# Squares summed over partitions in three bf16 parts instead of one f32 product, in a hybrid decoder block

## The reference

```python
h = rmsnorm(x, norm_g)
q_g, k_g, v_g, gk_lr, gate_g, u_p, gate_p, q_m, gate_m = split(h @ w_in)
gk = log_sigmoid(gk_lr @ w_gk_up + b_gk) / 16
o_gla = rmsnorm(gla_chunked(q_g, k_g, v_g, gk), gla_norm_g) * silu(gate_g)   # 4 heads of 128, chunks of 64
o_pool = (multiscale_pool(u_p) @ pool_w) * pool_scale * silu(gate_p)         # windows 2, 4, 8, 16
o_mem = memory_attention(q_m, rmsnorm(mem), w_mem_kv) * silu(gate_m)         # 4 heads, 256 tokens
x = x + concat(o_gla, o_pool, o_mem) @ w_out
return rmsnorm(x, final_g)
```

## Time and profile before

| | |
|---|---|
| Median of 3 runs | 1385.68 us (1384.72 to 1386.30) |
| The profiled execution's own time | 1386.14 us |
| Its span, first to last instruction | 1384.3 us |
| Instructions | 35236 |
| Busy: PE, DVE, ACT, POOL | 98%, 58%, 54%, 27% |
| Mean granted TensorE clock | 0.998 |

### The profile page before, as it was taken

The page is one execution under the profiler, slowest core; times in us unless marked ns, Lnnn a source line. Parts: engine busy times, 40 slices in busy tenths (PEclk is TensorE's granted clock), DMA queues, the critical chain, the costliest instruction groups (busy, mean ns, idle before and its releaser), DMA issues.

```text
span 1384.3 us, 35236 instructions
## 1 busy us (share of the span) xinstructions
PE 1357.1 (98%) x14716; PEld 1015.7 (73%) x14716; DVE 796.9 (58%) x1524; ACT 753.6 (54%) x1380; POOL 370.7 (27%) x313
## 2 busy tenths in 40 slices
PE   6999999999999999999999999999999999999997
PEld 5788668576695968769586785958768596876953
DVE  5876567575554654554555555565555455555454
ACT  7886545655545464454646545464554556455352
POOL 2120164135323142332223223222332313233100
PEclk9999999999999999999999999999999999999999
DMA  9476556663673737456383654638366373745731
GB/s 387 174 209 214 213 183 215 199 242 137 203 255 94 275 107 260 183 180 240 95 294 123 242 201 147 251 97 290 132 209 249 116 265 97 262 177 183 254 83 46
DMA packets 143623, 269.31 MB, mean 195 GB/s; under 512 B 75137, under 2 KB 88705, under 8 KB 140417
## 3 DMA queue, kind: packets, MB, share of 16 engines
q1 hardware_dynamic: 142768, 266.20, 56.3%
q10 hardware_dynamic: 720, 1.06, 0.2%
HBM read 220.03 MB, written 30.41 MB: 181 GB/s over the span
## 4 chain that ended last, share of the span: by engine, by line
PE 94%; DVE 3%; ACT 2%; DMA 1%; issue 0%; SPq 0%; DVEq 0%; ACTq 0%
PE bank L665 34%; PE bank L704 33%; PE bank L683 10%; PE bank L892 2%; PE bank L918 2%; PE bank L912 2%; PE bank L926 2%; PE bank L971 2%; PE bank L994 2%; PE bank L903 1%; PE bank L780 1%; PE bank L876 1%; DMA out_parts<-fg 1%; PE bank L607 1%; DVE arena L1578 1%; PE bank L764 1%
## 5 line engine op out<-in xcount | busy, mean ns | idle before, releaser
L665 PE MATMUL bank<-ring,arena 128*128 128x512 f16 x1440 | 318.4, 379 | 0.0
L665 PEld LDWEIGHTS bank<-ring,arena 128*128 128x128 f16 x1440 | 138.5, 98 | 165.6 <-issue 5.9
L704 PE MATMUL bank<-arena,ring 128*128 128x128 f16 x4032 | 237.1, 219 | 0.0
L704 PE MATMUL bank<-arena,wres 128*128 128x128 f16 x4032 | 237.0, 219 | 0.0
L704 PEld LDWEIGHTS bank<-arena,ring 128*128 128x128 f16 x4032 | 228.4, 98 | 5.2 <-DVE arena L1556 1.9
L704 PEld LDWEIGHTS bank<-arena,wres 128*128 128x128 f16 x4032 | 227.7, 98 | 2.5 <-issue 2.5
L665 PE MATMUL bank<-wv,arena 128*128 128x512 f16 x768 | 170.2, 382 | 1.1 <-DVE wv L1542 1.1
L2029 POOL TENSOR_TENSOR arena<-arena 128x1024 f32<-128x1024 f32 (+2 forms) x42 | 64.8, 1543 | 355.1 <-ACT arena L1042 352.9
L665 PEld LDWEIGHTS bank<-wv,arena 128*128 128x128 f16 x768 | 75.5, 98 | 91.3 <-issue 2.3
L2037 POOL TENSOR_TENSOR arena<-arena 128x1024 f16<-128x1024 f32 x32 | 67.5, 2131 | 200.1 <-ACT arena L1060 200.1
L1637 DVE SCALAR_TENSOR_TENSOR arena<-bank,sca,arena 128x512 f32<-128x512 f32 x60 | 45.0, 749 | 111.1 <-DMA arena<-in_x 92.2
(11 more groups left out here) (247 smaller groups left out, 2004.6 us busy)
## 6 DMA issues: line engine op xcount, KB each, us to landing
ring<-out_parts SPq DMA_DIRECT2D x120, 512.0 KB, 5.5
ring<-gate_parts SPq DMA_DIRECT2D x92, 512.0 KB, 5.8
ring<-side_parts SPq DMA_DIRECT2D x92, 512.0 KB, 6.5
arena<-in_xt SPq DMA_DIRECT2D x16, 1024.0 KB, 6.8
arena<-in_x SPq DMA_DIRECT2D x32, 512.0 KB, 4.4
out<-arena SPq DMA_DIRECT2D x31, 512.0 KB, 2.9
arena<-in_w_out SPq DMA_DIRECT2D x16, 512.0 KB, 5.4
out_parts<-arena SPq DMA_DIRECT2D x6, 512.0 KB, 6.7
```

What stands on the lines that cost most here:

```text
L665: mm = nc.tensor.matmul(ap, lhs, rhs, start=k == 0 and n == 0, stop=(k, n) == last)
L704: mm = nc.tensor.matmul(ap, w[:, p, k, j * P:(j + 1) * P], x_part(r, b)[:, k, :], start=fresh and j == 0 and k == 0 and n == 0, stop=k == ...
```

## The change

For the heads in blocks 1 to 14 and for the next x in blocks 4 to 14 the f32 squares are split into three bf16 numbers each (high part, middle part, rest), and three bf16 products with a bf16 matrix of ones are summed in PSUM in place of the one f32 product. For the heads ACT squares PSUM a second time with a bf16 output (`o_part[p][0]`, after waiting for the block's transposes, whose source lies in the same memory), DVE subtracts it from `osq`, ACT copies the difference to bf16 (`o_part[p][1]`), DVE subtracts again into `o_part[p][2]`. The order is: on ACT square and high part of each head in turn, then both middle parts, ahead of the copies SG3 and SG1; on DVE both first subtractions and both second ones, ahead of the third row add. For the next x the same four steps work on 256 columns: on ACT the high part stands before PM's second copy and the middle part behind it; on DVE the subtractions stand before and behind PM's `add_12`. The matrix `ident16`, which nothing read, gives way to `ones16`.

```diff
--- before.py
+++ after.py
@@ -123,7 +123,7 @@
         wlr = sb("wlr", [P, KT, 2 * RANK], F16)
         arena = sb("arena", [P, O_END // 4], F32)
         ident = sb("ident", [P, P], F32)
-        ident16 = sb("ident16", [P, P], F16)
+        ones16 = sb("ones16", [P, P], BF16)
         ones = sb("ones", [P, P], F32)
         causal = sb("causal", [P, P], F32)
         keep = sb("keep", [P, TB], BF16)
@@ -188,6 +188,7 @@
         kd = view(O_KD, [NPAIR, TB], F32)
         ke = view(O_KE, [NPAIR, TB], F32)
         osq = [view(o, [2, TB], F32) for o in (O_KD, O_KE)]
+        o_part = [[view(O_T + 3072 * p + 1024 * n, [2, TB], BF16) for n in range(3)] for p in range(2)]
         v = view(O_V, [NT, 512], F32)
         gate = view(O_GATE, [KT, TB], F32)
         mhl = view(O_MHL, [2, KT, TB], F16)
@@ -218,6 +219,7 @@
         pwb = view(O_QM, [2, P], F32)
         rmem = view(O_QM + 1024, [NMEM], F32)
         msq = sq
+        x_sum = [sq[:, 4 + n, :].bitcast(BF16)[:, 0:TB] for n in range(3)]
         sums = xs[:, 1, :, :, :].rearrange("p r b c -> p (r b c)")
         shade = {QK: wres[:, 0:2, :].rearrange("p s c -> p (s c)")[:, 0:4 * (512 + RANK)].rearrange(
                      "p (k c) -> p k c", k=4),
@@ -351,8 +353,10 @@
             sem(n) for n in ("sT_ok", "max_ok", "nmax_ok", "rs_ok", "s_ok", "xn_ok", "og_ok",
                              "mix_g", "mix_m", "mix_p", "mmax_ok", "m_lo"))
 
+        xsq_hi, xsq_rest, xsq_mid, xsq_lo = (sem(n) for n in ("xsq_hi", "xsq_rest", "xsq_mid", "xsq_lo"))
         w_sum, halo_ok, sq_add, p_lo, x_lo, m_all, s_carry, sg_ok = (
             sem(n) for n in ("w_sum", "halo_ok", "sq_add", "p_lo", "x_lo", "m_all", "s_carry", "sg_ok"))
+        osq_hi, osq_rest, osq_mid, osq_lo = (sem(n) for n in ("osq_hi", "osq_rest", "osq_mid", "osq_lo"))
         m_st, sc_ok, cut_ok = (sem(n) for n in ("m_st", "sc_ok", "cut_ok"))
         d_tail = [sem(f"d_tail{t}") for t in range(NT)]
         half_max, y_gain, y_end = (sem(n) for n in ("half_max", "y_gain", "y_end"))
@@ -606,6 +610,14 @@
                 pe.wait_ge(sq_add, 3 * (n + 1))
                 nc.tensor.matmul(bank[3][:, 0:TB], ones[:, :], sq[:, 0, :], start=True, stop=True).then_inc(pe_rb, 1)
 
+            def rms_parts(n):
+
+                pe.wait_ge(xsq_mid, n - WHOLE)
+                pe.wait_ge(xsq_lo, n - WHOLE)
+                for k in range(3):
+                    mm = nc.tensor.matmul(bank[3][:, 0:TB], ones16[:, :], x_sum[k], start=k == 0, stop=k == 2)
+                mm.then_inc(pe_rb, 1)
+
             def total(g):
 
                 pe.wait_ge(w_sq, 2 * (g + 1))
@@ -848,7 +860,7 @@
                     phase(i, PM, 2)
                     pe.wait_ge(ad[GG], 4 * (i + 1))
                     if not last:
-                        rms_sum(i + 1)
+                        rms_parts(i + 1)
                     pe.wait_ge(ad[QK], 4 * (i + 1))
                     values(0).then_inc(pe_v, 1)
                     values(1).then_inc(pe_v, 1)
@@ -922,9 +934,16 @@
 
                 def head_ms(p):
 
-                    pe.wait_ge(o_sq, 2 * i + p + 1)
-                    nc.tensor.matmul(bank[6 + p][:, :], ones[:, :], osq[p], start=True,
-                                     stop=True).then_inc(pe_msq, 1)
+                    if first or last:
+                        pe.wait_ge(o_sq, 2 * i + p + 1)
+                        nc.tensor.matmul(bank[6 + p][:, :], ones[:, :], osq[p], start=True,
+                                         stop=True).then_inc(pe_msq, 1)
+                        return
+                    pe.wait_ge(osq_mid, 2 * i + p - 1)
+                    pe.wait_ge(osq_lo, 2 * i + p - 1)
+                    for n in range(3):
+                        mm = nc.tensor.matmul(bank[6 + p][:, :], ones16[:, :], o_part[p][n], start=n == 0, stop=n == 2)
+                    mm.then_inc(pe_msq, 1)
 
                 def quarter(n):
                     if not first:
@@ -1332,7 +1351,13 @@
                     act.wait_ge(ad[GG], 4 * (i + 1))
                     early_copies(i, PM)
                     second_copy(i, UM)
+                    if not last:
+                        act.wait_ge(sq_add, 3 * (i + 2))
+                        nc.scalar.activation(x_sum[0], sq[:, 0, :], ACT.Copy).then_inc(xsq_hi, 1)
                     second_copy(i, PM)
+                    if not last:
+                        act.wait_ge(xsq_rest, i - WHOLE + 1)
+                        nc.scalar.activation(x_sum[1], sq[:, 0, :], ACT.Copy).then_inc(xsq_mid, 1)
                     third_copy(i, UM)
                     third_copy(i, PM)
                     qm_split()
@@ -1427,8 +1452,17 @@
                     if first:
                         act.wait_ge(cp[GG if p == 0 else PM], 4)
                         silu(p, GG if p == 0 else PM)
+                    elif not last:
+                        for turned in d_turn:
+                            act.wait_ge(turned, 32 * (i + 1))
+                        nc.scalar.activation(o_part[p][0], bank[b][:, :].rearrange("p (a t) -> p a t", a=2),
+                                             ACT.Square).then_inc(osq_hi, 1)
                 if first:
                     nc.scalar.preload_act_table_set(EXP_LN)
+                elif not last:
+                    for p in range(NPAIR):
+                        act.wait_ge(osq_rest, 2 * i + p - 1)
+                        nc.scalar.activation(o_part[p][1], osq[p], ACT.Copy).then_inc(osq_mid, 1)
                 if not last and not is_whole(i + 1):
                     x_mixed(i + 1, SG3)
                     x_mixed(i + 1, SG1)
@@ -1800,7 +1834,13 @@
                     mixed_lo(i - 1)
                     add_11(i, PM)
                     add_12(i, UM)
+                    if not last:
+                        dve.wait_ge(xsq_hi, i - WHOLE + 1)
+                        nc.vector.tensor_tensor(sq[:, 0, :], sq[:, 0, :], x_sum[0], ALU.subtract).then_inc(xsq_rest, 1)
                     add_12(i, PM)
+                    if not last:
+                        dve.wait_ge(xsq_mid, i - WHOLE + 1)
+                        nc.vector.tensor_tensor(x_sum[2], sq[:, 0, :], x_sum[1], ALU.subtract).then_inc(xsq_lo, 1)
                     add_2(i, UM)
                     add_2(i, PM)
 
@@ -1936,6 +1976,20 @@
                     norm_rows(i - 1, 0)
                 if not last:
                     dve.wait_ge(xn_ok, 2 * (i + 2))
+                def osq_rest_of(p):
+                    dve.wait_ge(o_sq, 2 * i + p + 1)
+                    dve.wait_ge(osq_hi, 2 * i + p - 1)
+                    nc.vector.tensor_tensor(osq[p], osq[p], o_part[p][0], ALU.subtract).then_inc(osq_rest, 1)
+
+                def osq_lo_of(p):
+                    dve.wait_ge(osq_mid, 2 * i + p - 1)
+                    nc.vector.tensor_tensor(o_part[p][2], osq[p], o_part[p][1], ALU.subtract).then_inc(osq_lo, 1)
+
+                if not first and not last:
+                    osq_rest_of(0)
+                    osq_rest_of(1)
+                    osq_lo_of(0)
+                    osq_lo_of(1)
                 if not last:
                     rows(2)
                 if first:
@@ -2019,7 +2073,7 @@
                                     pattern=[[1, P]], channel_multiplier=-1).then_inc(ident_ok, 1)
             pool.wait_ge(ident_ok, 4)
             nc.gpsimd.memset(causal[0:64, 64:128], 0.0).then_inc(built, 1)
-            nc.gpsimd.tensor_copy(ident16[:, :], ident[:, :]).then_inc(built, 1)
+            nc.gpsimd.memset(ones16[:, :], 1.0).then_inc(built, 1)
 
             def fold_rows(n0):
 
```

## The result

The changed kernel takes 1388.63 us (median of 13 runs, 1387.26 to 1390.73), the kernel before 1385.09 us (median of 13, 1384.19 to 1388.45) beside it. The ratio is 1.0022, with a 95% interval of 1.0015 to 1.0030: slower by 3.0 us by the ratio (2.1 to 4.2), by 3.5 us by the medians. 1388.4 us had been forecast.

What follows compares the result with a forecast made beforehand. TensorE, busy 98% of the span, was taken to bound the kernel. 10.6 us lost in blocks 1 and 2 less 7.9 gained elsewhere gave +2.7 on the median 1385.68, so 1388.4 us, range 1376.5 to 1393.0.

Steps and rivals of the forecast that it cites:

- TensorE's gain: Head sums in blocks 1 to 14 shorten by 0.51 us a block, next-x sums in blocks 4 to 14 by 0.16.
- Rival (d): On TensorE, three bf16 products cost what the f32 pass costs; the 7.9 us gain falls away, 1396 us; chance 0.05.
- The x chain: Blocks 4 to 14: ACT and DVE split x before TensorE's next-x sum, 0.3 us to spare, no cost.
- Rival (c): Low part of x late for TensorE's sum in blocks 4 to 14, 0.3 to 0.8 us a block; chance 0.12.
- The heads in blocks 3 to 14: Head subtractions end 3.3 us before TensorE asks; the spare before the logits shrinks to 0.39 us; no stall.
- The turns in blocks 1 and 2: New DVE subtractions alternate with GpSimd's weight combinations, 2.77 us a turn; TensorE stands 1.9 and 2.8 us.
- Rival (b): Blocks 1 and 2 don't stand, subtractions find gaps between GpSimd's operations; all is gained, 1376.8 us; chance 0.15.
- The clock: After the stands, one fall of TensorE's granted clock in each of blocks 1 and 2, 1.6 us on QK products.
- Rival (a): Turns in blocks 1 and 2 as said but the clock holds: 1385.3 us, no change; chance 0.16.
- the other bound: No fall of the clock in blocks 1 and 2, put at 3.1 us less.
- The sum: Blocks 1 and 2 lose 4.8 and 5.8 us, together 10.6; less 7.9 gained elsewhere, net +2.7 us.

Runs made afterwards that it cites:

- the run with late combinations: Changed kernel, but GpSimd's weight combinations wait for both head products of the block before, and plain copies replace DMA transposes: 1379.70 us, ratio 0.9965.

## Why the prediction was right, point by point

- **TensorE's gain.** x: 0.16 us a block forecast and measured. Heads: 0.51 forecast, 0.42 measured. This term was mis-sized: six products were put at 6 x 0.216 = 1.30 us, and the pair holds TensorE 1.39. The price of f16 held for bf16: the three of the first head take 0.65 in block 4 (the fourth product begins at 459.68). The last three hold TensorE 0.74 in blocks 1 and 2 (from 196.74 to 197.48), where they can be read apart, so 0.09 us lies between them and the low-rank product. What it is was not separated by a run. Over 12 blocks it made 7.9 us into 6.8. Rival (d), bf16 products as dear as f32, falls with these rows.
- **The x chain.** It passed with 0.5 us to spare, 0.3 forecast. In block 4 of the changed kernel the fold ends at 415.39; the high part, both subtractions and the window sum between them:

```profile
415.42 0.42 ACT L1356 ACTIVATE arena<-arena 128x256 bf16<-128x256 f32 x1 [3.16 <-POOL arena L2083]
...
415.87 0.84 DVE L1839 TENSOR_TENSOR arena<-arena 128x256 f32<-128x256 f32 x1 [3.09 <-ACT arena L1356]
...
417.20 0.74 DVE L1843 TENSOR_TENSOR arena<-arena 128x256 bf16<-128x256 f32 x1
...
415.35 1.09 POOL L2160 TENSOR_TENSOR arena<-arena 128x542 f32<-128x542 f32 x1
416.51 1.14 POOL L2162 TENSOR_TENSOR arena<-arena 128x538 f32<-128x538 f32 x1
```

  Both subtractions wait a turn, as forecast (0.84 and 0.74 us for 256 columns, where 0.4 was estimated without one), and the last is done at 417.94 for 418.46. Rival (c), slower by this chain, falls: no stand.
- **The heads in blocks 3 to 14.** No stand. In block 4 the last subtractions end at 455.78, 3.25 us before TensorE asks at 459.03; 3.3 were forecast. The copy that releases the logits ended at 464.59, the logits began at 465.00: 0.41 to spare, 0.39 forecast.

```profile
454.31 1.47 DVE L1986 TENSOR_TENSOR arena<-arena 128x512 bf16<-128x512 f32 x2
...
464.11 0.48 ACT L1204 ACTIVATE arena<-bank,sca 128x256 f32<-128x256 f32 x1 [0.60 <-DVE arena L1940]
465.00 1.08 PE L792 MATMUL bank<-arena,up 128*128 128x256 f32 x4
```

- **The turns in blocks 1 and 2.** Stands of 1.9 and 2.8 us were forecast; they were 1.77 and 2.73, 1.78 and 2.72. One turn was forecast at 2.77 us; two subtractions take 5.59, 2.8 each. The two blocks agree with each other within 0.01 us, so the mechanism was right here and not only the total. Rival (b), no turns, falls with the trace, and the run with late combinations shows that the turns are the cause, not only beside it.
- **The clock.** A fall in each, 1.6 us: 1.3 and 1.6 measured. That these falls come from the stands is read from the trace, and from the run with late combinations, where stands and falls are gone together; the falls were not tried apart from the stands. Rival (a), stands without falls, is out by the profiled execution; of the 13 runs none has a mean clock above its 0.997, and none is under 1387.26 us, where (a) gave 1385.3. That bound has a slip: the prediction's own logits times with and without a fall differ by 1.4 and 1.6 us, so the other bound was 3.0 us less and not 3.1; it moves no chance.
- **The sum.** +4.8 and +5.8 forecast for the two blocks, +4.5 and +5.9 measured. The net of +2.7 came out as +3.6 by the traces: 1.1 us less gain on the heads, 0.2 us less loss in the two blocks. By the medians it was +3.5, an error of 0.8 us. The median of before beside it was 0.6 us under the one that the forecast started from, which hid most of this. So it is luck that 1388.4 came within 0.2 us of 1388.63, where 0.8 us had been the honest miss; the mechanism and the sign are not luck.

## What to carry to other kernels

Before a DVE operation with two SBUF inputs is added, look in every stage for what GpSimd does at that time: where it has a row of long operations, each new one waited here for one of these whole (2.8 us for 0.7), and all that stands behind it in DVE's queue came later by as much. A change that is good in 12 of 14 blocks can lose in the other two more than it gains; left out there, the same change gives 0.995 (with copies for the transposes; with the transposes it was not run). A semaphore that holds GpSimd back moves the loss to whoever waits for GpSimd's results, so follow these to their last user first, DMA queue included.

## What the runs showed of the hardware

In the run with late combinations a scan takes turns too: two scans of 256 columns, 1.27 us together in the kernel before, take 5.41 us beside the combinations, and DVE's other operations with two SBUF inputs behind them 2.7 and 3.4 for 0.7 and 1.3.

```profile
208.37 5.41 DVE L1714 TENSOR_TENSOR_SCAN arena<-keep,arena 128x256 f32<-128x256 bf16 x2
213.82 2.66 DVE L1718 TENSOR_TENSOR arena<-arena 128x512 f32<-128x512 f32 x1
216.40 3.37 DVE L1561 SCALAR_TENSOR_TENSOR arena<-wres,sca,arena 128x1024 f16<-128x1024 f32 x1
```

The granted clock did not fall at every stand of 2 to 3 us. At 153.3 us it fell with a stand of 2.1 us in the profiled execution of before, and not with 2.3 us at the same place in that of after. The run with late combinations has both cases in one execution: no fall at the 2.8 us stand that ends at 254.31, and one at the stand of 2.45 us in the tail, which is as long in the kernels before and after and costs no fall there. In windows of 1 us:

```profile
254.00:255.00 1.00, 0.69 (x4) 1.00 1.04 426
1350.00:1351.00 1.00, 1.00 (x4) 0.50 0.00 0
```

The same fall in the tail is in the profiled execution without the heads of blocks 1 and 2. So one fall more or less, 1.4 to 1.7 us, can be part of the spread between executions, and a forecast that takes a fall for a single stand rests on chance.
